# A fused two-block kernel on one core: large arrays at multiples of 2048 bytes, blocks of L stored block-wise and loaded by one transfer, every DMA issued by SyncE

## Chip, core and metric

The kernel runs on one core of a Trainium2 chip. The metric is the device time of one execution in microseconds; lower is better. Three runs of the kernel before the change are at hand, and one profiled execution, whose times count from the start of its span.

## What is computed

Two transformer blocks run one after the other on one sequence of 256 tokens with 2048 channels, all in float32. The first has chunked attention beside a multi-scale pool, and a gated feed-forward with a small convolution (`w_in`, `w_o`, `w_up`, `w_down`). The second has an RWKV-7 mixer and then a differential attention (`a_w_in`, `a_w_out`, `w_k_shared`, `w_v_shared`, `b_w_qg`, `b_w_out`). What matters here is the RWKV-7 part, whose recurrence over the tokens is

```
def step(S, inp):
    r_t, w_t, k_t, v_t, kk_t, a_t = inp
    sa = jnp.einsum('bhvk,bhk->bhv', S, kk_t)
    S = (S * w_t[:, :, None, :]
         - sa[..., None] * (kk_t * a_t)[:, :, None, :]
         + v_t[..., None] * k_t[:, :, None, :])
    y = jnp.einsum('bhvk,bhk->bhv', S, r_t)
    return S, y
```

for 32 heads of 64 channels. `a` is a sigmoid of a low-rank product (rank 96), the decay comes from a second one, and `kk` is `k` times a gain, normalized over each head by the root of its sum of squares.

## The kernel before

**Products.** Every large product is made from weights that are streamed from memory in units of 128 x 4 x 256 floats (512 KB; some of 384 KB). Each weight is split into two float32r parts: ScalarE copies `raw_w` into `w_hi` (L1046, in the woven stage L1336), VectorE writes `w_lo = raw_w - w_hi` (L1495, L1879) into the place of `raw_w`. The activations are split alike (`A..H`, `A..L`, side by side in one buffer). TensorE takes for each 128 x 128 block of a unit one matmul of `w_hi` on 512 columns (both parts, L636) and one of `w_lo` on 256 columns (the high part, L637): a unit is 8 such pairs. There are 8 places for raw units and 4 for `w_hi`. So SyncE may issue the weights of unit n when TensorE has finished unit n - 8, and ScalarE may split unit n when TensorE has finished unit n - 4. Each engine runs through its own program in order and waits at semaphores.

**The woven stage.** The products of the RWKV-7 mixer for `r`, `v` and `g` are 96 units (`NW`), written out unit by unit in one loop over n on each engine, and everything that the recurrence needs beforehand is put between the units at given n:
- The low-rank products: `lora_first` behind unit 7 of TensorE and `lora_second` (L794, matmuls L803) behind unit 15. The second makes 16 groups into three banks, and a bank comes free when ScalarE has taken the sigmoid of it (`sigmoids`, L1271, placed at n == 19, behind the square root of the norms). VectorE takes the reciprocal of the norms at n == 19 (`kk_rows`), and the result is wanted behind unit 20.
- For each of the 16 feature tiles f, with `prep_at(f) = 20 + 9f//4`, TensorE makes the triangular blocks of L for 8 (chunk, head) pairs (`lt_product`, L832, behind unit `prep+8`), ScalarE copies them to one of two small buffers (`lt_out`, L1302, at `prep+10`, which first waits until the store of tile f - 2 has landed), and SyncE stores them to `lt_dram` (`store_lt`, L475, at `prep+20`; two DMAs).
- L is then wanted with its 128 (tile, chunk, head) triples on the partitions. SyncE loads it with `load_lt` (L457), two DMAs of 8 partitions a tile: the first 15 tiles behind the weights of n = 73, the last one at n = 74.
- VectorE inverts the two 32 x 32 diagonal blocks of all 128 matrices at once in 31 steps of two operations each (`inverse_step`, L1861; the lines L1867 and L1870). The first step waits for all loads. The steps are spread over 21 units from n = 67:

```
        INVERSE_FROM = 67

        def inverse_steps(n):

            return range(max(0, n - INVERSE_FROM) * 31 // 21, min(max(0, n + 1 - INVERSE_FROM), 21) * 31 // 21)
```

Within its turn n VectorE first makes `w_lo` of the unit, then an evacuation (L1533, every fourth n), then the work of the tiles, then the steps of the inverse.
- Behind the weights of the last unit SyncE waits for the inverse, stores it (L520) and loads it block by block for the recurrence (`load_t`, L471), which follows the woven stage and uses small matmuls (L863).

**Queues.** SyncE issues the weights, the inputs, the scratch traffic and the output. GpSimd issues the constants at the start (L548, L549, L556), four side arrays of the attention (L565, behind the split of the first operand), the pool's weights (L568, behind the first product) and the distances and an expansion matrix (L613, L615).

**Memory.** The arrays are laid one behind another in each partition: the parameters (702 floats), the constants (896 floats), `w_lo`/`raw_w`, `w_hi`, two small arrays of 48 floats together, `x`, and so on.

## Time and profile before

| | |
|---|---|
| median of 3 runs | 2550.43 us (2547.89 to 2554.88) |
| profiled execution | 2553.74 us, of it span 2551.9 us |
| TensorE busy | 2353.8 us, 15826 matmuls |
| VectorE busy | 1490.3 us |
| ScalarE busy | 1093.7 us |
| GpSimd busy | 52.6 us |
| mean DMA traffic | 149 GB/s |

Busy time of TensorE is from the start of a matmul to its modelled end, and successive matmuls overlap, so a full TensorE is not one at its peak. "Granted clock" is the share of full clock that TensorE got: 1.00 is 2.4 GHz, and the lower level is 1.2 GHz. The chain that ended last goes back from the last instruction to what released it, or to the one before it on its engine. In the rows, PE is TensorE, DVE VectorE, ACT ScalarE, and SPq the queue of SyncE.

### The profile page before, as it was taken

The numbers are of one execution on the slowest core, as the hardware profiler recorded it, in microseconds if no ns is written. First come the engines' busy times: TensorE is split into PE (matmuls) and PEld (weight loads), VectorE is DVE, ScalarE is ACT, GpSimd is POOL, SyncE is SP. The second block draws the span as 40 slices with busy tenths as digits, with TensorE's granted clock in tenths as the row PEclk, the third lists the DMA queues.
The fourth block names the chain that finished last, engine by engine and source line by source line (L and its number), as shares of the span: only waits on it lengthen the run. The fifth ranks groups of instructions, "written<-read, shape, count | busy, mean of one in ns | idle before, by whom it ended". The sixth has DMA issues, their size and how long they took to land.

```text
span 2551.9 us, 41854 instructions
## 1 busy us (share of the span) xinstructions
PE 2353.8 (92%) x15826; PEld 1983.6 (78%) x15826; DVE 1490.3 (58%) x2024; ACT 1093.7 (43%) x1489; POOL 52.6 (2%) x61
## 2 busy tenths in 40 slices
PE   7997988999999999996999995999898899999797
PEld 6886777888888888885877775888477788887486
DVE  5555457775577657758735684722454544444754
ACT  4443435554444434442446452322333544444533
POOL 0003000000000000000000000000010000000100
PEclk9998999999999999997999997999889999999898
DMA  7662444565666656562644456400344455665052
GB/s 251 186 184 74 133 132 139 183 188 184 186 185 185 188 183 188 167 188 85 212 141 140 147 161 117 148 9 11 101 140 131 149 189 182 188 184 162 1 163 68
DMA packets 395775, 379.69 MB, mean 149 GB/s; under 512 B 41889, under 2 KB 394145, under 8 KB 394961
## 3 DMA queue, kind: packets, MB, share of 16 engines
q1 hardware_dynamic: 394690, 373.72, 47.9%
q0 software_dynamic: 976, 4.46, 0.5%
q8 instruction: 75, 1.23, 0.2%
q14 instruction: 34, 0.28, 0.0%
HBM read 370.79 MB, written 7.34 MB: 148 GB/s over the span
## 4 chain that ended last, share of the span: by engine, by line
PE 84%; DVE 9%; ACT 2%; issue 1%; DMA 1%; SPq 1%; POOL 0%; DVEq 0%; ACTq 0%; POOLq 0%
PE acc L636 48%; PE acc L637 24%; PE acc L863 3%; PE aux L863 2%; PE aux L676 1%; PE aux L686 1%; DVE w_lo L1879 1%; PE aux L809 1%; DVE w_lo L1495 1%; SPq L461 1%; DVE inverse L1870 1%; PE aux L803 1%; PE aux L786 1%; DVE outer L1867 1%; DVE y L1576 1%
## 5 line engine op out<-in xcount | busy, mean ns | idle before, releaser
L1495 DVE TENSOR_TENSOR w_lo<-raw_w,w_hi 128x1024 fp32r<-128x1024 f32 (+1 forms) x592 | 710.3, 1209 | 633.3 <-ACT w_hi L1046 631.5
L1046 ACT ACTIVATE w_hi<-raw_w 128x1024 fp32r<-128x1024 f32 (+1 forms) x592 | 618.4, 1049 | 852.6 <-PE acc L637 848.9
L636 PE MATMUL acc<-h,w_hi 128*128 128x512 f32 x1920 | 683.2, 399 | 23.7 <-DVE w_lo L1495 16.4
L637 PE MATMUL acc<-h,w_lo 128*128 128x256 f32 x1920 | 541.4, 282 | 0.0
L636 PEld LDWEIGHTS acc<-h,w_hi 128*128 128x128 f32 x1920 | 363.2, 189 | 113.8 <-issue 24.1
L636 PE MATMUL acc<-x_split,w_hi 128*128 128x512 f32 x1024 | 363.5, 399 | 8.7 <-DVE x_split L2004 8.7
L637 PEld LDWEIGHTS acc<-h,w_lo 128*128 128x128 f32 x1920 | 362.6, 189 | 0.0
L637 PE MATMUL acc<-x_split,w_lo 128*128 128x256 f32 x1024 | 288.4, 282 | 0.0
L636 PE MATMUL acc<-ff,w_hi 128*128 128x512 f32 x704 | 249.5, 398 | 1.0 <-DVE ff L1702 1.0
L636 PEld LDWEIGHTS acc<-x_split,w_hi 128*128 128x128 f32 x1024 | 193.3, 189 | 56.8 <-issue 9.0
L636 PE MATMUL acc<-xs_a,w_hi 128*128 128x512 f32 x512 | 190.6, 412 | 25.6 <-DVE xs_a L1753 21.3
L636 PE MATMUL acc<-xs_b,w_hi 128*128 128x512 f32 x512 | 186.9, 406 | 27.6 <-DVE w_lo L1879 26.9
L637 PE MATMUL acc<-ff,w_lo 128*128 128x256 f32 x704 | 197.8, 281 | 0.0
L637 PEld LDWEIGHTS acc<-x_split,w_lo 128*128 128x128 f32 x1024 | 193.1, 189 | 0.0
L636 PEld LDWEIGHTS acc<-ff,w_hi 128*128 128x128 f32 x704 | 132.4, 188 | 34.0 <-DVE ff L1702 1.3
L1879 DVE TENSOR_TENSOR w_lo<-raw_w,w_hi 128x1024 fp32r<-128x1024 f32 x96 | 116.5, 1222 | 70.9 <-ACT w_hi L1336 69.8
L637 PE MATMUL acc<-xs_a,w_lo 128*128 128x256 f32 x512 | 145.9, 285 | 0.0
L637 PE MATMUL acc<-xs_b,w_lo 128*128 128x256 f32 x512 | 145.0, 283 | 0.0
L636 PEld LDWEIGHTS acc<-xs_a,w_hi 128*128 128x128 f32 x512 | 98.4, 192 | 58.7 <-issue 31.1
L636 PEld LDWEIGHTS acc<-xs_b,w_hi 128*128 128x128 f32 x512 | 97.6, 191 | 57.9 <-DVE w_lo L1879 28.5
L1336 ACT ACTIVATE w_hi<-raw_w 128x1024 fp32r<-128x1024 f32 x96 | 100.2, 1053 | 85.0 <-PE acc L637 72.4
L637 PEld LDWEIGHTS acc<-ff,w_lo 128*128 128x128 f32 x704 | 132.2, 188 | 0.1
(304 smaller groups left out, 2942.2 us busy)
## 6 DMA issues: line engine op xcount, KB each, us to landing
raw_w<-in_w_up SPq DMA_DIRECT2D x176, 512.0 KB, 3.6
raw_w<-in_a_w_in SPq DMA_DIRECT2D x128, 512.0 KB, 3.6
raw_w<-in_w_in SPq DMA_DIRECT2D x64, 512.0 KB, 3.6
raw_w<-in_w_down SPq DMA_DIRECT2D x64, 512.0 KB, 3.5
raw_w<-in_b_w_qg SPq DMA_DIRECT2D x64, 512.0 KB, 3.6
raw_w<-in_w_o SPq DMA_DIRECT2D x32, 512.0 KB, 3.6
raw_w<-in_a_w_out SPq DMA_DIRECT2D x32, 512.0 KB, 4.3
raw_w<-in_w_k_shared SPq DMA_DIRECT2D x32, 512.0 KB, 3.6
```

The lines of the kernel that those rows point to most:

```text
L461: sp.dma_start(LT[8 * f:8 * f + 8, b, :, :], lt_dram[8 * f:8 * f + 8, b * H:(b + 1) * H, b * H:(b + 1) * H])\
L636: pe.matmul(out, wh, op[:, kt, :, :].rearrange("p h t -> p (h t)"), start=first, stop=False)
L637: mm = pe.matmul(out[:, 0:T], wl, op[:, kt, 0, :], start=False, stop=last)
L676: mm = pe.matmul(bank[:, 0:T], ONES, x[:, ds(4 * i + k, 1), :], start=(isinstance(i, int) and i == 0 and k == 0), stop=last)
L686: mm = pe.matmul(AUX[0][:, 0:T], ONES, SQB[0][:, j % 2, k, :], start=(j + k == 0), stop=(j + k == 6))
L786: mm = pe.matmul(AUX[w][0:LORA, 0:T], W1S[:, w, k, :], x[:, k, :], start=(k == 0), stop=(k == KD - 1))
L803: mm = pe.matmul(AUX[(0, 1, 3)[j % 3]][:, x * T:(x + 1) * T], W2S[:, w, f * P:(f + 1) * P], LOW[:, w, :], start=True, stop=True)
L863: mm = pe.matmul(bank[64 * h_:64 * h_ + 64, i * n:(i + 1) * n], lhs(h_, i), rhs(h_, i), start=(start and i == 0), stop=(stop and i == 3))
L1046: act.activation(WHI[:, q, 0:ku, :], RAWW[:, u, 0:ku, :], ACT.Copy).then_inc(hi_made, 1)
L1336: act.activation(WHI[:, n % 4, :, :], RAWW[:, slot, :, :], ACT.Copy).then_inc(hi_made, 1)
L1495: dve.tensor_tensor(WLO[:, u, 0:ku, :], RAWW[:, u, 0:ku, :], WHI[:, q, 0:ku, :].bitcast(F32), ALU.subtract)\
L1879: dve.tensor_tensor(WLO[:, slot_of(n), :, :], RAWW[:, slot_of(n), :, :], WHI[:, n % 4, :, :].bitcast(F32), ALU.subtract)\
```

## The change

The change has six parts. (1) The two small arrays go ahead of the weights, with a filler of 368 floats, and the reserve for DMAs that software describes shrinks from 8192 to 2048 bytes; the large arrays then start at multiples of 2048 bytes. (2) `lt_dram` has the shape of `LT`, (128, 2, 32, 32). A tile is stored with four DMAs, one for each head and diagonal block, three units earlier; all of `LT` is loaded with one DMA behind the weights of n = 71, once all stores have landed. (3) The inverse starts at n = 69 and its 31 steps are spread over 20 units. (4) The DMAs of GpSimd are issued by SyncE: the constants ahead of the first weights, `scan` and the side arrays behind the weights of `w_in`, the pool's weights behind the first 8 units of `w_o`, the last two behind the weights of `a_w_out`. (5) ScalarE takes the sigmoids at n == 18 and the square root after them. (6) The waits are adapted.

```
@@ -170,11 +170,12 @@
         HEADSEL = CF[:, CCOL["headsel"]:CCOL["headsel"] + CHUNK]
         PAIRSEL = CF[:, CCOL["pairsel"]:CCOL["pairsel"] + CHUNK]
         STACK = CF[:, CCOL["stack"]:CCOL["stack"] + CHUNK]
+        OMU, OKA = sb(root, "one_minus_mu", [P, 2 * KD]), sb(root, "one_minus_k_a", [P, KD])
+        sb(root, "pad_to_10k", [P, 368])
         with ExitStack() as same_place:
             WLO = sb(same_place, "w_lo", [P, RAW, KU, UNIT_COLS], F32R)
         RAWW = sb(root, "raw_w", [P, RAW, KU, UNIT_COLS])
         WHI = sb(root, "w_hi", [P, SPL, KU, UNIT_COLS], F32R)
-        OMU, OKA = sb(root, "one_minus_mu", [P, 2 * KD]), sb(root, "one_minus_k_a", [P, KD])
         X = sb(root, "x", [P, KD, T])
         FOLD = sb(root, "fold", [P, 4, T])
 
@@ -402,15 +403,16 @@
 
         PREP = {prep_at(f): f for f in range(KD)}
         PAIRS = {pair_at(s_, p): (s_, p) for s_ in (1, 2) for p in range(8)}
-        INVERSE_FROM = 67
+        INVERSE_FROM, INVERSE_OVER = 69, 20
 
         def inverse_steps(n):
 
-            return range(max(0, n - INVERSE_FROM) * 31 // 21, min(max(0, n + 1 - INVERSE_FROM), 21) * 31 // 21)
+            done = [min(max(0, x - INVERSE_FROM), INVERSE_OVER) * (H - 1) // INVERSE_OVER for x in (n, n + 1)]
+            return range(*done)
 
         def by_chunk(x):
             return x.rearrange("p (c t) -> p c t", c=NCH)
-        lt_dram, t_dram, x_dram = dram("lt_scratch", (P, CHUNK, CHUNK)), dram("t_scratch", (P, 2, H, H)), dram("x_scratch", (P, KD, T))
+        lt_dram, t_dram, x_dram = dram("lt_scratch", (P, 2, H, H)), dram("t_scratch", (P, 2, H, H)), dram("x_scratch", (P, KD, T))
 
         def small(m, n):
 
@@ -445,8 +447,22 @@
             for q in range(4):
                 sp.dma_start(X[:, 4 * q:4 * q + 4, :], h["x_t"][4 * q * P:4 * (q + 1) * P].rearrange("(k p) t -> p k t", p=P))\
                   .then_inc(x_in[q], 16)
+            sp.dma_start(CF[:, 0:NFIX], h["consts"][:, 0:NFIX]).then_inc(const_in, 16)
+            sp.dma_start(CF[:, NFIX:], h["consts"][:, CCOL["tri"]:CCOL["expand"]]).then_inc(const_in, 16)
             weights(8, lambda i, b: (w_in, i * 512 + b * 256))
-            weights(4, lambda i, b: (h["w_o"][0], i * 512 + b * 256))
+
+            sp.dma_start(SCAN[:, :], h["consts"][:, CCOL["scan"]:CCOL["scan"] + T]).then_inc(scan_in, 16)
+            sp.wait_ge(operand, 4)
+            band0 = CCOL["band"]
+            for dst, src in ((HANK[:, :, :], h["bias_rows"]),
+                             (FLIP[:, :], h["consts"][:, CCOL["flip"]:CCOL["flip"] + P]),
+                             (BAND[:, :, :], h["consts"][:, band0:band0 + 2 * T].rearrange("p (q t) -> p q t", q=2)),
+                             (INVC[:, :, :], h["consts"][:, CCOL["invcount"]:CCOL["invcount"] + 4 * T].rearrange("p (g t) -> p g t", g=4))):
+                sp.dma_start(dst, src).then_inc(side, 16)
+            weights(1, lambda i, b: (h["w_o"][0], i * 512 + b * 256))
+            sp.wait_ge(acc_free, 4 + 32)
+            sp.dma_start(POOLW[:, :, :, :], h["pool_w"][0].rearrange("g (c p) d -> p g c d", p=P)).then_inc(pool_w_in, 16)
+            weights(3, lambda i, b: (h["w_o"][0], i * 512 + (512 + b * 256)))
             for t0, tiles in GROUPS:
                 weights(tiles // 2, lambda i, b: (w_up, i * 256 + (t0 * P + b * FF)))
                 weights(4, lambda i, b: (w_down, i * 512 + b * 256), ku=tiles // 4, kt0=t0)
@@ -454,13 +470,6 @@
 
             sp.wait_ge(x_ready, 8)
             sp.dma_start(x_dram, X[:, :, :]).then_inc(x_spilled, 16)
-            def load_lt(f):
-
-                sp.wait_ge(lt_stored[f % 2], 32 * (f // 2 + 1))
-                for b in range(2):
-                    sp.dma_start(LT[8 * f:8 * f + 8, b, :, :], lt_dram[8 * f:8 * f + 8, b * H:(b + 1) * H, b * H:(b + 1) * H])\
-                      .then_inc(inv_in, 16)
-
             def load_t(n):
                 g, c = STEPS[n]
                 m = n % 2
@@ -474,9 +483,11 @@
 
             def store_lt(f):
                 sp.wait_ge(lt_ready, f + 1)
+                dst = lt_dram[8 * f:8 * f + 8].rearrange("(c h) b s t -> h b s c t", h=2)
                 for hh in range(2):
-                    dst = lt_dram[8 * f:8 * f + 8].rearrange("(c h) s t -> h s c t", h=2)[hh]
-                    sp.dma_start(dst, (XS, US)[f % 2][64 * hh:64 * hh + 64, :, :]).then_inc(lt_stored[f % 2], 16)
+                    for b in range(2):
+                        at = 64 * hh + H * b
+                        sp.dma_start(dst[hh, b], (XS, US)[f % 2][at:at + H, :, H * b:H * b + H]).then_inc(lt_stored[f % 2], 16)
 
             def woven_weights(n):
 
@@ -508,13 +519,12 @@
                 if n == 16:
                     lora_weights_2()
                 woven_weights(n)
-                if n - 20 in PREP:
-                    store_lt(PREP[n - 20])
-                if n - 21 in PREP and n - 21 > 51:
-                    load_lt(PREP[n - 21])
-                if n == 73:
-                    for f in range(15):
-                        load_lt(f)
+                if n - 17 in PREP:
+                    store_lt(PREP[n - 17])
+                if n == 71:
+                    for even_odd in lt_stored:
+                        sp.wait_ge(even_odd, 64 * KD // 2)
+                    sp.dma_start(LT[:, :, :, :], lt_dram).then_inc(inv_in, 16)
             seen(unit_done, NW)
             sp.wait_ge(inverted, 1)
             sp.dma_start(t_dram, TT[:, :, :, :]).then_inc(t_stored, 16)
@@ -531,6 +541,11 @@
             sp.wait_ge(bon_done, KD)
             sp.dma_start(X[:, :, :], x_dram).then_inc(x_back, 16)
             weights(4, lambda i, b: (h["a_w_out_2"][0], i * 512 + b * 256))
+
+            sp.wait_ge(gn_ready, KD)
+            sp.dma_start(DIST[:, :, :], h["consts"][:, CCOL["dist"]:CCOL["dist"] + 2 * T].rearrange("p (q t) -> p q t", q=2))\
+                .then_inc(dist_in, 16)
+            sp.dma_start(EXP5[:, :], h["consts"][0:32, CCOL["expand"]:CCOL["expand"] + D // 2]).then_inc(dist_in, 16)
             for w in (h["w_k_shared_2"], h["w_v_shared_2"]):
                 weights(4, lambda i, b: (w, i * 512 + b * 256))
             weights(8, lambda i, b: (h["b_w_qg_2"][0], i * 512 + b * 256))
@@ -545,28 +560,14 @@
         @block.gpsimd
         def _(pool):
             seen = Counts(pool)
-            pool.dma_start(CF[:, 0:NFIX], h["consts"][:, 0:NFIX]).then_inc(const_in, 16)
-            pool.dma_start(CF[:, NFIX:], h["consts"][:, CCOL["tri"]:CCOL["expand"]]).then_inc(const_in, 16)
             pool.sem_inc(unit_done, RAW)
             pool.sem_inc(acc_free, 4)
             pool.sem_inc(sq_free, 2)
             pool.sem_inc(sc_free, 2)
 
 
-            pool.dma_start(SCAN[:, :], h["consts"][:, CCOL["scan"]:CCOL["scan"] + T]).then_inc(scan_in, 16)
             pool.memset(LOW[LORA:LORA + 1, :, :], 1.0).then_inc(low_one, 1)
             pool.wait_ge(low_one, 1)
-            pool.wait_ge(operand, 4)
-            band0 = CCOL["band"]
-            for dst, src in ((HANK[:, :, :], h["bias_rows"]),
-                             (FLIP[:, :], h["consts"][:, CCOL["flip"]:CCOL["flip"] + P]),
-                             (BAND[:, :, :], h["consts"][:, band0:band0 + 2 * T].rearrange("p (q t) -> p q t", q=2)),
-                             (INVC[:, :, :], h["consts"][:, CCOL["invcount"]:CCOL["invcount"] + 4 * T].rearrange("p (g t) -> p g t", g=4))):
-                pool.dma_start(dst, src).then_inc(side, 16)
-
-            pool.wait_ge(acc_free, 4 + 32)
-            pool.dma_start(POOLW[:, :, :, :], h["pool_w"][0].rearrange("g (c p) d -> p g c d", p=P)).then_inc(pool_w_in, 16)
-
             def link(ins):
                 ins.then_inc(gstep, 1)
                 pool.wait_ge(gstep, seen(gstep))
@@ -609,10 +610,6 @@
                 pool.tensor_tensor(gnt(1, f), gnt(1, f), G4[:, f, :], ALU.mult).then_inc(gn_gated, 1)
 
 
-            pool.wait_ge(gn_ready, KD)
-            pool.dma_start(DIST[:, :, :], h["consts"][:, CCOL["dist"]:CCOL["dist"] + 2 * T].rearrange("p (q t) -> p q t", q=2))\
-                .then_inc(dist_in, 16)
-            pool.dma_start(EXP5[:, :], h["consts"][0:32, CCOL["expand"]:CCOL["expand"] + D // 2]).then_inc(dist_in, 16)
             for n in range(8):
                 pool.wait_ge(o_out, n + 1)
                 pool.tensor_tensor(Q5[:, 2 * n:2 * n + 2, :], Q5[:, 2 * n:2 * n + 2, :], G5[:, 2 * n:2 * n + 2, :], ALU.mult).then_inc(o_gated, 1)
@@ -1269,12 +1266,12 @@
                 act.activation(KFR[:, f % 3, :], K[:, f, :], ACT.Square, scale=PV[:, c:c + 1]).then_inc(kk_sq, 1)
 
             def sigmoids():
-                act.wait_ge(kk_summed, KD)
-                act.activation(INVR[:, :], AUX[2][0:32, 0:T], ACT.Sqrt).then_inc(kk_norm, 1)
                 for j in range(KD):
                     act.wait_ge(lora_done, j + 1)
                     act.activation((KAP, BET)[j % 2][:, j // 2 * 2:j // 2 * 2 + 2, :],
                                    AUX[(0, 1, 3)[j % 3]][:, :].rearrange("p (x t) -> p x t", x=2), ACT.Sigmoid).then_inc(sig_ready, 1)
+                act.wait_ge(kk_summed, KD)
+                act.activation(INVR[:, :], AUX[2][0:32, 0:T], ACT.Sqrt).then_inc(kk_norm, 1)
 
             def k_factor(f):
                 c = COL["a_k_a_2"] + f
@@ -1303,7 +1300,7 @@
                 p = f % 2
                 act.wait_ge(lt_done, f + 1)
                 if f >= 2:
-                    act.wait_ge(lt_stored[p], 32 * (f // 2))
+                    act.wait_ge(lt_stored[p], 64 * (f // 2))
                 act.activation((XS, US)[p][:, :, :], by_chunk(AUX[1][:, 0:T]), ACT.Copy)\
                    .then_inc(lt_ready, 1)
 
@@ -1345,7 +1342,7 @@
                 if 8 <= n < 16:
                     kk_square(2 * (n - 8))
                     kk_square(2 * (n - 8) + 1)
-                if n == 19:
+                if n == 18:
                     sigmoids()
                 if n - 10 in PREP:
                     lt_out(PREP[n - 10])
@@ -1861,7 +1858,7 @@
             def inverse_step(s_):
                 n, r = s_ + 1, H - 1 - s_
                 if s_ == 0:
-                    dve.wait_ge(inv_in, 32 * KD)
+                    dve.wait_ge(inv_in, 16)
                     dve.wait_ge(inv_init, 1)
                 o = OUTER[:, 0:2 * n * r].rearrange("p (b j t) -> p b j t", b=2, j=n)
                 link(dve.tensor_tensor(o, LT[:, :, s_:s_ + 1, s_ + 1:].broadcast_to([P, 2, n, r]),
@@ -2098,7 +2095,7 @@
     rows = x["rel_bias"][0][:, np.clip(distance, -P, P) + P]
     arrays["bias_rows"] = np.ascontiguousarray(rows.transpose(1, 0, 2))
 
-    nc = _bacc.Bacc("TRN2", target_bir_lowering=False, num_devices=1, dynamic_dma_scratch_size=8192)
+    nc = _bacc.Bacc("TRN2", target_bir_lowering=False, num_devices=1, dynamic_dma_scratch_size=2048)
     h = {n: nc.dram_tensor("in_" + n, a.shape, F32, kind="ExternalInput").ap() for n, a in arrays.items()}
     h["out"] = nc.dram_tensor("out_t", (D, T), F32, kind="ExternalOutput").ap()
     program(nc, h)
```

## Rows read from the trace of the kernel before

**Rows 1.** The profile's page: the chain that ended last, by engine.

```profile
PE 84%; DVE 9%; ACT 2%; issue 1%; DMA 1%; SPq 1%; POOL 0%; DVEq 0%; ACTq 0%; POOLq 0%
```

**Rows 2.** Waits of the whole span: total us, times, longest us.

```profile
DVE outer L1867 <- DMA lt_blocks<-lt_scratch: 31.3, 1, 31.3
PE acc L636 <- DVE w_lo L1879: 29.0, 6, 25.5
```

**Rows 3.** Timeline of SyncE's queue, 1538 to 1585 us: start, length, what.

```profile
1539.17 1.26 SPq L479 DMA_DIRECT2D lt_scratch<-wkv_x  x2
...
1547.12 18.56 SPq L461 DMA_DIRECT2D lt_blocks<-lt_scratch  x30
```

**Rows 4.** Timeline of VectorE, 1573 to 1578 us; in brackets the idle before.

```profile
1574.19 0.23 DVE L1867 TENSOR_TENSOR outer<-lt_blocks,inverse 128x62 f32<-128x62 f32 x1 [31.31 <-DMA lt_blocks<-lt_scratch]
```

**Rows 5.** Timeline of TensorE, 1549 to 1586 us.

```profile
1575.99 0.79 PE L636 MATMUL acc<-xs_b,w_hi 128*128 128x512 f32 x1 [25.55 <-DVE w_lo L1879]
...
1576.79 0.63 PE L636 MATMUL acc<-xs_b,w_hi 128*128 128x512 f32 x1
...
1577.43 0.63 PE L636 MATMUL acc<-xs_b,w_hi 128*128 128x512 f32 x1
...
1582.33 0.40 PE L636 MATMUL acc<-xs_b,w_hi 128*128 128x512 f32 x1
1582.57 0.28 PE L637 MATMUL acc<-xs_b,w_lo 128*128 128x256 f32 x1
1582.69 0.39 PE L636 MATMUL acc<-xs_b,w_hi 128*128 128x512 f32 x1
```

**Rows 6.** Timeline of TensorE, 1340 to 1368 us: the second low-rank product.

```profile
1343.42 2.86 PE L803 MATMUL aux<-lora_low,raw_w 97*128 97x256 f32 x12
1351.18 14.24 PE L803 MATMUL aux<-lora_low,raw_w 97*128 97x256 f32 x52 [4.90 <-ACT r_kappa L1276]
```

**Rows 7.** Timelines of ScalarE and TensorE, 1430 to 1440 us.

```profile
1435.05 0.39 ACT L1307 ACTIVATE wkv_u<-aux 128x256 f32<-128x256 f32 x1 [5.25 <-DMA lt_scratch<-wkv_u]
...
1438.79 0.51 PE L636 MATMUL acc<-xs_a,w_hi 128*128 128x512 f32 x1 [1.74 <-DVE w_lo L1879]
```

**Rows 8.** DMA issues: count, KB each, median us from issue to landing.

```profile
lt_scratch<-wkv_x SPq DMA_DIRECT2D x16, 64.0 KB, 3.3
...
t_scratch<-inverse SPq DMA_DIRECT2D x1, 1024.0 KB, 6.5
inverse_blocks<-t_scratch SPq DMA_DIRECT2D x64, 16.0 KB, 1.8
```

**Rows 9.** VectorE's groups, 1574 to 1636 us: count | busy us, mean ns.

```profile
L1879 DVE TENSOR_TENSOR w_lo<-raw_w,w_hi 128x1024 fp32r<-128x1024 f32 x22 | 26.9, 1224 | 0.7
L1870 DVE TENSOR_TENSOR inverse<-inverse,outer 128x62 f32<-128x62 f32 (+15 forms) x31 | 16.4, 528 | 1.1
L1867 DVE TENSOR_TENSOR outer<-lt_blocks,inverse 128x62 f32<-128x62 f32 (+15 forms) x31 | 16.2, 522 | 31.7 <-DMA lt_blocks<-lt_scratch 31.3
L1533 DVE SCALAR_TENSOR_TENSOR silu_g<-acc,fold 128x512 f32<-128x512 f32 x5 | 3.4, 684 | 0.0
```

**Rows 10.** Waits of SyncE's queue from 1370 to 1550 us.

```profile
SPq L491 <- PE acc L637: 135.3, 49, 3.7
```

**Rows 11.** Timeline of ScalarE, 1341 to 1366 us: a split, table load, sigmoid.

```profile
1342.20 1.06 ACT L1336 ACTIVATE w_hi<-raw_w 128x1024 fp32r<-128x1024 f32 x1 [0.18 <-DMA raw_w<-in_a_w_in]
...
1349.23 1.28 ACT L1276 ACT_TABLE_LOAD   x1
...
1363.72 0.60 ACT L1276 ACTIVATE beta<-aux 128x512 f32<-128x512 f32 x1 [0.27 <-PE aux L803]
```

**Rows 12.** Timeline of ScalarE, 13 to 16 us: the first weights.

```profile
13.94 1.06 ACT L1046 ACTIVATE w_hi<-raw_w 128x1024 fp32r<-128x1024 f32 x1 [2.31 <-DMA raw_w<-in_w_in]
15.43 1.06 ACT L1046 ACTIVATE w_hi<-raw_w 128x1024 fp32r<-128x1024 f32 x1 [0.44 <-DMA raw_w<-in_w_in]
```

**Rows 13.** The page's costliest groups: matmuls on the first operand.

```profile
L636 PE MATMUL acc<-h,w_hi 128*128 128x512 f32 x1920 | 683.2, 399 | 23.7 <-DVE w_lo L1495 16.4
```

81 lines of the change are left out of this document (40 added, 41 removed).

## The prediction, made before the changed kernel was run

> **What bounds the kernel now.** I read the page's first and fourth parts, the table of waits, and then, in the stretch that the waits pointed at, the timelines of TensorE, VectorE, ScalarE and of the queue on SyncE. The page says that TensorE is busy for nine tenths of a span of 2551.9 us and carries 84% of the chain that ended last [rows 1]. So an edit pays only where TensorE stands still, or where it makes TensorE itself faster. The waits show one such place above all: 31.3 us in which VectorE waits for the load of `lt_blocks`, and in its wake 29.0 us, all its times together, in which TensorE waits for `w_lo` [rows 2].
>
> The queue shows why. Behind unit 73 it issues 30 of the 32 loads of `lt_blocks` in 18.56 us [rows 3]; weights and the last two loads come after them. VectorE wants these blocks in its turn for unit 67, for the first of 31 elimination steps, and in its program order the `w_lo` of unit 68 stands behind them. It gets them at 1574.19 [rows 4]. TensorE stands still for 25.55 us and starts again at 1575.99 [rows 5]. It comes back at the lower of its two levels, 1.2 GHz: one pair of matmuls (a 128x512 on `w_hi`, a 128x256 on `w_lo`) takes 0.64 us from start to start; some 6 us later, at 2.4 GHz, it is 0.35 us [rows 5] (2.82 us for the 8 pairs of a unit, so 0.353 more exactly).
>
> The second place is the second low-rank product, L803: 12 matmuls in 2.86 us, a gap of 4.90 us until the first sigmoid, then 52 in 14.24 us [rows 6]. A third is small: one store of `lt_scratch` landed late, ScalarE waited 5.25 us for it, and TensorE lost 1.74 us [rows 7].
>
> **The change, part by part.**
>
> *Blocks loaded by one transfer.* 32 loads go, one of 1 MB comes. The scratch array now has the shape of `LT`, so it is one contiguous row for each of 128 partitions. The nearest row is the 1 MB store of the inverse, 6.5 us to landing [rows 8]. Count from the end of TensorE's unit 62. SyncE then issues unit 70 and the last four stores; two of today's, of 256 pieces each, take 1.26 us to issue [rows 3], so four with half the pieces some 2 us. They land 3.3 us behind issue [rows 8], so all is stored about 5.5 us after unit 62. The load then lands 6.5 us later, at 12 us. VectorE asks for it behind `w_lo` of unit 69, which cannot be made before unit 65 is done (3 x 2.82 = 8.5 us) plus 1.05 us for `w_hi` and 1.2 us for `w_lo`: 10.7 us. It waits 1 to 2 us, while TensorE has units 66 to 69 ready, some 6 us of cover beyond that. No stall is left. This takes out 25.55 us. It also takes out the slow restart: from 1575.99 to 1582.33 only 10 pairs ran, in 6.34 us instead of 3.53 us: 2.8 us.
>
> *31 steps over 20 units from 69, instead of 21 from 67.* In the stretch of the steps VectorE has 16.4 + 16.2 us of steps, 22 subtractions of 1.224 us and 3.4 us of joins [rows 9], with hardly a gap: it is full. For 21 units it needs 16.4 + 16.2 + 25.7 + 3.4 = 61.7 us (less small overlaps) where TensorE needs 59.3; for 20 units 60.5 against 56.5. The 4 us that it falls behind are under the lead that it starts with, which the stalled kernel did not have. Before, TensorE had three gaps of some 0.4 us here; I take 0.7 us afterwards in place of 1.3. Bounds: a gain of 1.3, a loss of 3. The inverse ends one unit, 2.8 us, later. Its store (6.5 us) and the first loads (1.8 us) [rows 8] still end before TensorE's last unit, because SyncE issues that store only behind the weights of unit 95, that is, when unit 87 is done, with 8 units left.
>
> Stall, restart and steps: 25.55 + 2.8 + 0.6 = 29.0 us.
>
> *Stores by blocks, earlier.* Two stores of 256-byte pieces become four of 128-byte pieces (64 issues for 32); the number of pieces is the same. SyncE issues them three units earlier (17 instead of 20 behind the tile's first). By then ScalarE's copy is done, since it follows the product behind unit `prep+8` and SyncE's place is the end of unit `prep+9`: nothing new blocks weights behind it. The issues add 16 x 0.7 = 11 us to a queue that waits 135.3 us for TensorE between 1370 and 1550 [rows 10]. That is the cover. The nearest row for such pieces is `inverse_blocks`: 128-byte pieces, 16 KB, 1.8 us [rows 8]. The buffer is wanted again two tiles on, 3.5 units or more behind the issue, over 12 us. So the 1.74 us go. The Trainium skill, "DMA: Bandwidth & Descriptors", Specifications, speaks against the smaller pieces: below 512 bytes a DMA does not run at line rate. By that rule a store would land no sooner though it carries half the bytes; at the old 3.3 us the sum stays as it is.
>
> *Sigmoids at n = 18, the square root behind them.* Before, ScalarE waits for the weights of unit 19, splits them, evacuates, loads a table, takes the root and loads a second table from 1349.23 on [rows 11]; the first sigmoid follows at 1350.5, 7 us behind the first product. Now the sigmoids follow the split of unit 18 (1342.20 + 1.06) and one table load of 1.28 us [rows 11]: first one at 1344.6, done at 1345.1, before TensorE's fourth group (three banks are free at the start). After that ScalarE keeps a pace of 0.865 us (0.60 and 0.27 us idle) [rows 11], so TensorE sets it: 16 x 0.865 = 13.9 us. Before it was 22.0 us from 1343.42 to 1365.4. Gain 7.7 us (4.9 of gap, the rest is the low level after it). What is late next: the root, then the reciprocal on VectorE, both wanted behind unit 20; they are ready near 1365, unit 20 ends near 1371. The split of unit 19 comes out near 1362.5 with its unit due at 1365.5. Bounds: 4.9 to 8 us.
>
> *DMAs from GpSimd to SyncE.* At the start SyncE issues the two constant loads between x and the weights: two issues of 0.55 us, a gap-free queue behind 2 MB of x. TensorE starts when the first weights, landed at 13.94 [rows 12], are split. The same bytes stand ahead of them, but for the 128 KB of `scan`, which now come later, worth 0.4 us at the 0.5 MB in 1.5 us of the weights' landings [rows 12]. I take -0.4 us, bounds -1.5 to +1.5. The other loads follow the last `w_in` weights (25 us before the attention wants them), the pool's waits for the same evacuation as before, and the last two are wanted 450 us later: nothing.
>
> *Arrays at multiples of 2048 bytes.* No row of this trace sets two start addresses against each other. What the trace shows is that a matmul on `w_hi` takes 399 ns on the mean over the 1920 of `h` [rows 13], as it does in the woven stage at the upper level [rows 5], though what VectorE, ScalarE and the DMAs do beside it differs. I take 0. The bounds are wide and are the rivals C and D. The Trainium skill, "DMA: Bandwidth & Descriptors", How a descriptor splits into AXI transactions, would favour it: pieces off a 256-byte boundary cost extra beats, an estimated 36 for 32 on a 1 KB row. By that the weights at the start would land 1.3 us sooner; elsewhere DMA is hidden.
>
> **Sum:** 29.0 + 1.7 + 7.7 + 0.4 = 38.8 us. The profiled execution took 2553.74 us for a span of 2551.9; it would take 2514.9. The median of the runs is 3.3 us lower, 2550.43, so the forecast is 2511.6 us.
>
> **Rivals.**
> A. *The blocks still come late.* The load hangs on all 64 stores, the last of them issued behind unit 70. If store and load together take 22 us, not 12, VectorE drains its cover and TensorE stops again for 4.5 us and then runs behind a full VectorE: 12 us of the 29.0 are lost, 2524. For it: VectorE is full; against it: the two landings measured [rows 8]. 8%.
> B. *The sigmoids give nothing*, because the root that now comes last is waited for, or ScalarE's late split of unit 19 is: 2519. Two to four us of slack speak against it. 6%.
> C. *The matmuls get faster by alignment.* At 2.4 GHz 768 columns take 320 ns, the pair takes 353 [rows 5]. If all of that went, the 5440 pairs of the large products would give 180 us: 2332. Against it: the excess grows with the columns (0.24 and 0.12 us for 512 and 256) [rows 5], as a rate does and a bad start address doesn't. 6%.
> D. *Slower: with all large arrays at the same place modulo 2048, TensorE's reads of operand and weights, or those of other engines, collide.* Place: every pair. It decides from 38.8 us / 5440 = 7 ns a pair, 2% of 353. For a price, the only row with slower pairs is the low level; a twentieth of the way from 353 to 640 is 14 ns, 76 us in all less the gains: 2588. Against it: today's constant rate beside changing company. 5%.
> E. *The wait stays*: another semaphore, for instance that of the stores, holds VectorE or SyncE as long as before; only the sigmoids and the small stall are gained: 2541. 3%.
>
> **Numbers.** The forecast case has 72%, its own range is 2505 to 2519. With A and B the range is 2500 to 2526, which leaves out C, D and E. A measurement of this kernel tells 0.3% (7.7 us) from nothing: faster 0.93, same 0.03, slower 0.04.
>
> **What would show it.** In the profile afterwards: no wait of VectorE for `lt_blocks` over 3 us; no gap of TensorE over 2 us between unit 16 and unit 95 of the woven stage; one load of `lt_blocks` of 1 MB; L803's 64 matmuls in about 14 us at one clock; no wait of ScalarE for `lt_scratch`; the first `w_hi` near 13.5 us. A pair that is not 353 ns makes the prediction wrong in one way, a full VectorE with gaps in TensorE near units 78 to 88 in the other.

## The result, and the profile after

The changed kernel takes 2484.9 us (median of 4 runs, 2476.6 to 2492.0) against 2549.9 us before on the same chip (4 runs, 2547.9 to 2554.9): a ratio of 0.974, 95% interval 0.970 to 0.978. The forecast was 2511.6 us with a range from 2500, so the kernel is faster by 27 us more than I said and lies 15 us below my range. The profiled execution took 2489.8 us for a span of 2487.7. Two things are to be read: the steps that I had costed came out nearly as costed in their sum (40.3 us against 38.8, in the run with the old layout below), and the step that I had costed at nothing is worth 22 us or somewhat more.

First the steps that were costed. The page's chain by engine, against [rows 1]:

```profile
PE 87%; DVE 9%; ACT 2%; issue 1%; DMA 0%; POOL 0%; SPq 0%; DVEq 0%; ACTq 0%; POOLq 0%
```

The waits of the whole span (total, times, longest), against [rows 2]:

```profile
PE acc L633 <- DVE w_lo L1876: 0.8, 1, 0.8
...
DVE outer L1864 <- DMA lt_blocks<-lt_scratch: 0.2, 1, 0.2
```

31.3 us of waiting for `lt_blocks` have become 0.2 us, and in their wake TensorE's 29.0 us of waiting for `w_lo` have become 0.8. The queue on SyncE and VectorE after it (timelines of 1495 to 1520 us; [rows 3, 4] before):

```profile
1505.51 1.94 SPq L490 DMA_DIRECT2D lt_scratch<-wkv_u  x4
1507.91 0.39 SPq L502 DMA_DIRECT2D raw_w<-in_a_w_in  x1
1509.55 0.34 SPq L527 DMA_DIRECT2D lt_blocks<-lt_scratch  x1
...
1516.15 0.23 DVE L1864 TENSOR_TENSOR outer<-lt_blocks,inverse 128x62 f32<-128x62 f32 x1 [0.21 <-DMA lt_blocks<-lt_scratch]
```

From the issue of the last four stores to VectorE's first step are 10.6 us; I had worked out 12 us from unit 62 on. The page's DMA issues give the landings, against [rows 8]:

```profile
lt_blocks<-lt_scratch SPq DMA_DIRECT2D x1, 1024.0 KB, 6.6
t_scratch<-inverse SPq DMA_DIRECT2D x1, 1024.0 KB, 6.3
inverse_blocks<-t_scratch SPq DMA_DIRECT2D x64, 16.0 KB, 1.8
lt_scratch<-wkv_x SPq DMA_DIRECT2D x32, 16.0 KB, 2.6
```

The second low-rank product (timelines of TensorE, then of ScalarE, 1320 to 1340 us; [rows 6, 11] before) has its 64 matmuls in one piece. The first sigmoid comes 1.16 us behind the first of them, and the root is last:

```profile
1322.91 14.08 PE L800 MATMUL aux<-lora_low,raw_w 97*128 97x256 f32 x64
...
1322.74 1.28 ACT L1271 ACT_TABLE_LOAD   x1
1324.07 0.60 ACT L1271 ACTIVATE r_kappa<-aux 128x512 f32<-128x512 f32 x1
1324.94 0.60 ACT L1271 ACTIVATE beta<-aux 128x512 f32<-128x512 f32 x1 [0.27 <-PE aux L800]
...
1337.64 1.28 ACT L1274 ACT_TABLE_LOAD   x1
1338.93 0.38 ACT L1274 ACTIVATE kk_inverse_rows<-aux 32x256 f32<-32x256 f32 x1
```

Now the place where the rest of the gain is. The page's groups for the matmuls of `w_hi`, for the first operand [rows 13 before] and the last large one:

```profile
L633 PE MATMUL acc<-h,w_hi 128*128 128x512 f32 x1920 | 669.8, 393 | 23.0 <-DVE w_lo L1492 15.7
...
L633 PE MATMUL acc<-x_split,w_hi 128*128 128x512 f32 x1024 | 363.2, 400 | 8.6 <-DVE x_split L2001 8.6
```

On `h` a matmul has gone from 399 to 393 ns; on `x_split` it has not (400). The view by windows counts matmuls, and that is the sharper reading: it gives busy time (and count) of the line's matmuls and of its weight loads, the granted clock, the DMA share and GB/s. Line L636 before:

```profile
450.00:1050.00 600.00, 600.00 (x1699) 319.22 (x1698) 1.00 0.60 185
1990.00:2260.00 270.00, 270.00 (x765) 143.63 (x764) 1.00 0.60 185
```

Line L633 after:

```profile
450.00:1050.00 600.00, 600.00 (x1731) 323.62 (x1732) 1.00 0.61 188
1990.00:2260.00 270.00, 270.00 (x765) 143.62 (x765) 1.00 0.61 186
```

In the same 600 us TensorE takes 32 more pairs, at the same granted clock of 1.00 (2.4 GHz) and with nearly the same DMA share (0.61 against 0.60); in the other stretch it takes as many as before. From the start times: before, a pair is 353.3 ns from start to start, everywhere. After, it is either 346.7 ns (three pairs in 1040 ns) or 353.3 ns (three in 1060 ns), and the level holds without an exception through each stretch of 60 pairs or more in which TensorE isn't interrupted. The level can change between stretches without any fall of the clock: stretches of 63 pairs that start at 1185, 1209 and 1232 us run at 346.7, 353.4 and 346.7 ns, and the granted clock is 1.00 from 1170 to 1735 us. The mean over all pairs goes from 353.3 to 349.3 ns; times 5440 pairs that is 22 us.

### The profile page after: what moved, and what is told of

Same layout as the page of the kernel before. It is cut to its first block, busy times and chain, and to the rows that moved or that the text cites. A ratio compares the mean times of both kernels' runs of the same rounds, so it can differ in the third digit from the quotient of the medians.

```text
span 2487.7 us, 41832 instructions
## 1 busy us (share of the span) xinstructions
PE 2324.1 (93%) x15826; PEld 1970.7 (79%) x15826; DVE 1489.4 (60%) x2024; ACT 1092.7 (44%) x1489; POOL 46.7 (2%) x51
## 4 chain that ended last, share of the span: by engine, by line
PE 87%; DVE 9%; ACT 2%; issue 1%; DMA 0%; POOL 0%; SPq 0%; DVEq 0%; ACTq 0%; POOLq 0%
PE acc L633 49%; PE acc L634 25%; PE acc L860 3%; PE aux L860 3%; PE aux L673 1%; PE aux L806 1%; PE aux L683 1%; DVE w_lo L1492 1%; PE aux L800 1%; PE aux L783 1%; DVE y L1573 1%; PE aux L946 0%; DVE inverse L1867 0%; DVE diff_scores L2043 0%; DVE w_lo L1876 0%
## 5 line engine op out<-in xcount | busy, mean ns | idle before, releaser
L633 PE MATMUL acc<-h,w_hi 128*128 128x512 f32 x1920 | 669.8, 393 | 23.0 <-DVE w_lo L1492 15.7
L634 PE MATMUL acc<-h,w_lo 128*128 128x256 f32 x1920 | 537.7, 280 | 0.0
L633 PEld LDWEIGHTS acc<-h,w_hi 128*128 128x128 f32 x1920 | 361.1, 188 | 103.9 <-issue 23.4
L633 PE MATMUL acc<-x_split,w_hi 128*128 128x512 f32 x1024 | 363.2, 400 | 8.6 <-DVE x_split L2001 8.6
L634 PEld LDWEIGHTS acc<-h,w_lo 128*128 128x128 f32 x1920 | 364.1, 190 | 0.0
L634 PE MATMUL acc<-x_split,w_lo 128*128 128x256 f32 x1024 | 288.1, 281 | 0.0
L633 PE MATMUL acc<-ff,w_hi 128*128 128x512 f32 x704 | 245.3, 393 | 1.1 <-DVE ff L1699 1.1
L633 PEld LDWEIGHTS acc<-x_split,w_hi 128*128 128x128 f32 x1024 | 193.1, 189 | 57.3 <-issue 9.0
L633 PE MATMUL acc<-xs_a,w_hi 128*128 128x512 f32 x512 | 189.7, 412 | 23.6 <-DVE xs_a L1750 21.4
L634 PE MATMUL acc<-ff,w_lo 128*128 128x256 f32 x704 | 196.9, 280 | 0.0
L634 PEld LDWEIGHTS acc<-x_split,w_lo 128*128 128x128 f32 x1024 | 194.1, 190 | 0.0
L633 PE MATMUL acc<-xs_b,w_hi 128*128 128x512 f32 x512 | 183.4, 402 | 1.5 <-DVE w_lo L1876 0.8
L633 PEld LDWEIGHTS acc<-ff,w_hi 128*128 128x128 f32 x704 | 131.8, 187 | 30.9 <-DVE ff L1699 1.5
L1876 DVE TENSOR_TENSOR w_lo<-raw_w,w_hi 128x1024 fp32r<-128x1024 f32 x96 | 116.5, 1221 | 62.5 <-ACT w_hi L1333 61.1
L634 PE MATMUL acc<-xs_a,w_lo 128*128 128x256 f32 x512 | 145.2, 284 | 0.0
L634 PE MATMUL acc<-xs_b,w_lo 128*128 128x256 f32 x512 | 143.5, 280 | 0.0
L633 PEld LDWEIGHTS acc<-xs_a,w_hi 128*128 128x128 f32 x512 | 98.3, 192 | 56.4 <-issue 30.9
L634 PEld LDWEIGHTS acc<-ff,w_lo 128*128 128x128 f32 x704 | 132.9, 189 | 0.1
L633 PEld LDWEIGHTS acc<-xs_b,w_hi 128*128 128x128 f32 x512 | 96.2, 188 | 30.4 <-issue 5.5
```

The lines of the kernel that those rows point to most:

```text
L633: pe.matmul(out, wh, op[:, kt, :, :].rearrange("p h t -> p (h t)"), start=first, stop=False)
L634: mm = pe.matmul(out[:, 0:T], wl, op[:, kt, 0, :], start=False, stop=last)
L1876: dve.tensor_tensor(WLO[:, slot_of(n), :, :], RAWW[:, slot_of(n), :, :], WHI[:, n % 4, :, :].bitcast(F32), ALU.subtract)\
```

## The experiments

Levels below are of the pair, start to start. "Distance" is where the operands of the large products start minus where the weights start, in bytes modulo 256. The kernel before has the weights at 384 and the operands at 576 modulo 2048 (distance 192); the changed one has both at 0.

**The parts one by one.** First the layout alone, on the kernel before:

```
+        OMU, OKA = sb(root, "one_minus_mu", [P, 2 * KD]), sb(root, "one_minus_k_a", [P, KD])
+        sb(root, "pad_to_10k", [P, 368])
         with ExitStack() as same_place:
             WLO = sb(same_place, "w_lo", [P, RAW, KU, UNIT_COLS], F32R)
...
         WHI = sb(root, "w_hi", [P, SPL, KU, UNIT_COLS], F32R)
-        OMU, OKA = sb(root, "one_minus_mu", [P, 2 * KD]), sb(root, "one_minus_k_a", [P, KD])
...
-    nc = _bacc.Bacc("TRN2", ..., dynamic_dma_scratch_size=8192)
+    nc = _bacc.Bacc("TRN2", ..., dynamic_dma_scratch_size=4096)
```

> The kernel before with the large arrays at multiples of 2048 bytes and nothing else (reserve 4096 instead of 8192 bytes, so that the filler fits; weights start at 12,288). Theory (the start addresses set the rate of the matmul pairs): stretches with 346.7 ns a pair appear, the time falls by 15 to 30 us against before, ratio about 0.990 to 0.994. Rival (the pair rate comes from the other edits, the moved DMAs for instance): every pair stays at 353 ns and the time is that of before within 0.3%.

Measured: 2519.7 us (2512.6 to 2529.9) beside 2547.7 of before, ratio 0.988 (0.986 to 0.990). The mean pair is 349.2 ns. 28 us come from the layout alone: the fall is inside the 15 to 30 us that I expected, the ratio just under the 0.990 to 0.994 that I had written beside it. (This edit also halves the reserve; further down only pads move, and the levels move with them.) (The profiled execution, 2529.9 us, was the slowest of the four; its 4.1 ns a pair are 22 us.)

The reverse, the changed kernel with the arrays put back (no pad, the two small arrays behind `w_hi`, a DMA scratch of 8192):

> The changed kernel with the old layout (weights at 14,720, operands 576 bytes past a multiple of 2048). Theory: all pairs at 353 ns, time near the blind forecast, 2508 to 2516 us, ratio 0.984 to 0.987. Rival: pairs at 347 ns remain and the time stays near 2485 us.

Measured: 2507.3 us (2505.3 to 2509.1), ratio 0.984 (0.982 to 0.985), 353.3 ns in every stretch. This is the kernel that my sum described; it said 2511.6. Against the 2547.7 us of before beside it, 40.3 us are gained where the sum had 38.8. The first starts of some products say where the gain lies:

| first start, us | before | blocks alone | sigmoids alone | changed, old layout |
|---|---|---|---|---|
| L803's product | 1343.4 | 1340.3 | 1342.7 | 1340.8 |
| first blocks of L | 1405.9 | 1403.1 | 1397.3 | 1395.3 |
| scan, first product | 1661.7 | 1626.4 | 1653.6 | 1618.7 |
| end | 2551.9 | 2514.1 | 2543.8 | 2506.9 |

The stage of the sigmoids is 8.0 us shorter (62.5 to 54.5), the woven stage 32.4 us (255.8 to 223.4), what stands behind it 2.0 us, what stands ahead 2.6 us. Ahead of L803 the blocks alone, which change nothing there, came 3.1 us earlier too: these last two are the scatter of one execution.

Blocks alone (the one-transfer load, the stores by blocks, 20 units from 69, on the kernel before):

> The kernel before with the block-wise stores, the one load and the steps over 20 units from 69 alone. My sum gives 29.0 + 1.7 us: 2519 us, ratio 0.988, no gap of TensorE over 1 us in units 60 to 95. Rival (the wait for the blocks stays in another form): 2540 us or more.

Measured: 2517.2 us (2515.9 to 2518.4), ratio 0.988 (0.986 to 0.990), 30.4 us less than 2547.7.

Sigmoids alone (called at `n == 18`, the root behind them):

> The kernel before with the sigmoids at n == 18 and the root behind them alone. My sum gives 7.7 us: 2542 us, ratio 0.997, the 64 matmuls of the second low-rank product in 14 us without a gap. Rival (the stall at unit 67 swallows the gain, or the root is waited for): 2550 us.

Measured: 2543.2 us, 10 runs, ratio 0.998 (0.997 to 0.999). The stall of the blocks is all there, in TensorE's timeline:

```profile
1567.94 0.79 PE L636 MATMUL acc<-xs_b,w_hi 128*128 128x512 f32 x1 [25.75 <-DVE w_lo L1879]
```

Its profile shows 7.9 us gained in the stage itself, the medians 4.5 us (the interval allows 1.8 to 6.9, so 7.7 is outside). Where the difference goes I did not find; the moved DMAs have no run of their own. Both together are bounded: 2517.2 - 2507.3 = 9.9 us.

**Which address?** In each of the next runs only pads differ from the changed kernel. The first two move one side. The operands 576 bytes on:

```
         WHI = sb(root, "w_hi", [P, SPL, KU, UNIT_COLS], F32R)
+        sb(root, "pad_operands", [P, 144])
```

> The changed kernel with only the operands of the large products (x_split, mix, ff, wkv_out, h, xs_a, xs_b) moved by 576 bytes, back to their old place modulo 2048; w_hi and w_lo stay at multiples of 2048. Theory M (what counts is where the moving operand starts, since its 256 columns are the rows that TensorE streams... the operand is the stationary side or the moving side of every matmul alike): pairs of 353.3 ns throughout and some 2507 us, as with the old layout. Theory W (what counts is where the weights start): the fast stretches of 346.7 ns stay, the mean pair is near 349.3 ns and the time between 2476 and 2492 us. If each side gives a part: a mean pair between 349.3 and 353.3, some 2496 us.

The weights 384 bytes on, the operands at a multiple of 2048 as they were:

```
-        sb(root, "pad_to_10k", [P, 368])
+        sb(root, "pad_to_10k", [P, 368 + 96])
...
+        sb(root, "pad_operands", [P, 512 - 96])
```

> The mirror image: w_lo and w_hi start at 384 modulo 2048, their old place, and the operands stay at multiples of 2048. Theory W (the weights' start counts): pairs of 353.3 ns throughout, some 2507 us. Theory M (the operands' start counts): fast stretches of 346.7 ns stay, 2476 to 2492 us. A third reading, that both sides have to be aligned at once, gives 2507 us here and in the run with the operands moved.

Measured: 2508.0 us (2494.8 to 2513.6) and 2497.3 us (2494.2 to 2498.8). Neither theory holds. With the operands moved the levels are 348.9 and 353.3 ns; with the weights moved there is one level, 351.1 ns, in all stretches. It matters where both sides stand, taken together. The window view for the second, line L634:

```profile
450.00:1050.00 600.00, 600.00 (x1710) 320.88 (x1710) 1.00 0.61 187
1990.00:2260.00 270.00, 270.00 (x770) 144.43 (x769) 1.00 0.61 187
```

Then both sides moved together, by 1024, by 128 (`+ 32`), and by 576 bytes (`+ 144`):

```
-        sb(root, "pad_to_10k", [P, 368])
+        sb(root, "pad_to_10k", [P, 368 + 256])
```

> The changed kernel with its pad longer by 1024 bytes, so that all large arrays start at 1024 modulo 2048. If the multiple of 2048 itself matters: pairs of 353.3 ns, some 2507 us. If a smaller multiple (256, 512, 1024) is enough: nothing changes, mean pair near 349.3 ns and 2476 to 2492 us. I think the second likelier, 3 to 1.

> The changed kernel with its pad longer by 128 bytes: all large arrays start at 128 modulo 2048, which is where the old layout's weights stood modulo 256. If a multiple of 256 bytes or more is what counts: pairs of 353.3 ns throughout, some 2507 us. If a multiple of 128 or 64 is enough and it was the order of the arrays that mattered: near 349.3 ns, 2476 to 2492 us.

> The changed kernel with its pad longer by 576 bytes: weights and operands all start at 576 modulo 2048, the place of the operands in the old layout. If only the distance between weights and operands modulo 2048 counts: levels 346.7 and 353.3 ns as at 0, 128 and 1024, between 2476 and 2509 us. If the start address itself counts down to 64 bytes: another level, and with 353.3 throughout some 2507 us.

Measured: 2486.2 us (2482.1 to 2491.2), 2504.3 us (2493.4 to 2508.9) and 2495.7 us (2493.8 to 2500.5). All three have the two levels of the changed kernel, 346.7 and 353.3 ns, and differ in which stretches have which. So no multiple of 2048, 1024 or 256 is needed for the fast level to appear. But the times are not alike: 2482.1 to 2491.2 us with both at 1024, 2493.4 to 2508.9 with both at 128, run beside each other. In the profiles, the two longest stretches are both slow with both sides at 128 and at 576, while one of the two is fast at 1024. More on this under what stays open.

**Is the level fixed or drawn?** The changed kernel, the same program once more (no edit):

> The changed kernel once more, nothing in the program changed. Theory R (the level of the pair, 346.7 or 353.3 ns, is a state of a kernel with weights and operands at the same place modulo 2048 that is drawn anew at disturbances): the same two levels, but in other stretches than in the first profile; x_split, all slow there, may be fast here; any time between 2476 and 2492 us. Rival (the level is fixed by the addresses of each stage): the same stretches at the same levels, x_split at 353.3 and h at 346.7 ns, 2485 to 2492 us.

Measured: 2492.5 us. Line L633:

```profile
450.00:1050.00 600.00, 600.00 (x1699) 319.06 (x1698) 1.00 0.60 186
1990.00:2260.00 270.00, 270.00 (x780) 145.67 (x779) 1.00 0.62 190
```

The two stretches have changed places: 1699 where the first profile had 1731, and 780 where it had 765. The same program has the levels in other places, so they are not fixed by the addresses of a stage: the level is drawn when TensorE starts again and is then kept. The interruption can be very short: with the operands at 576, one pair that took 367 ns in place of some 349, at 1577.5 us, was enough to change 348.9 into 353.3 ns. Two stretches matter most, because nothing interrupts them: 1931 pairs from 392 us (12.9 us between the levels) and 1018 pairs from 1924 us (6.8 us). Draws of this size can make most of the scatter of the changed kernel, 2476.6 to 2492.5 us, but not all of it: from 349.2 to 350.5 ns, the mean pairs of the two profiled executions, are 7 us over 5440 pairs, and the executions are 2.7 us apart. The levels of the executions without a profile are not known.

**The distance.** Four more with only the operands moved, `pad_operands` being `[P, 64]`, `[P, 32]`, `[P, 48]` and `[P, 56]`:

> The changed kernel with only the operands moved by 256 bytes against the weights. If what counts is the distance of operands and weights modulo 256: as the changed kernel, levels 346.7 and 353.3 ns, 2476 to 2509 us. If it is the distance modulo 512 or more: a level in between (349 to 351 ns in some stretch, as at 384 and 576), 2494 to 2508 us.

> The changed kernel with only the operands moved by 128 bytes against the weights. If the distance modulo 128 or less counts: levels 346.7 and 353.3 ns, 2476 to 2509 us. If the distance modulo 256 or more counts: a level in between, 2494 to 2508 us.

> The changed kernel with only the operands moved by 192 bytes against the weights, the distance that the old layout has modulo 256. Theory D: 353.3 ns in every long run of pairs and 2505 to 2509 us, though weights and operands both stand at multiples of 64 and the weights at a multiple of 2048. Rival (aligned weights give part of the gain in themselves): a level under 353, 2490 to 2500 us.

> The changed kernel with only the operands moved by 224 bytes against the weights, 32 bytes short of the same place modulo 256. On a straight line from 346.7 ns at 0 by 2.22 ns for 64 bytes it would be 354.4 ns, some 2512 us; if the levels stop at 353.3 ns: some 2507 us; if it goes by nearness to 256: 347.8 ns and 2480 to 2508 us.

Measured: 2483.4 us (2479.4 to 2487.7), 2496.2 us (2493.8 to 2497.4), 2510.5 us (2504.3 to 2511.0) and 2501.7 us (2499.5 to 2506.1). At 256 the kernel behaves as at 0, and in the layouts below too the level goes by the distance modulo 256. At 192, the old distance, it is at 353.3 ns although the weights stand at a multiple of 2048 (the time is 1.5 us over the 2505 to 2509 that I expected): aligned weights alone give nothing. 128 is 351.1 ns again, as with the weights at 384 and the operands at 0, which is 128 modulo 256 too. And at 32 bytes (`[P, 8]`):

> The changed kernel with only the operands moved by 32 bytes against the weights. The lower level so far is 346.7 ns at distance 0, 348.9 at 64, 351.1 at 128 and 353.3 at 192, 2.22 ns for 64 bytes. If it goes in a straight line: 347.8 ns where the run is fast. If it goes in steps of 64 bytes: 346.7 or 348.9. Open is whether the upper level of 353.3 is drawn as well: with it 2480 to 2508 us, without it 2478 to 2484 us.

Measured: 2476.4 us (2474.1 to 2478.8), ratio 0.971 (0.969 to 0.973), and 346.7 ns in every long stretch. The slow level was not drawn once, and there is no 347.8 ns: the straight line of my expectation is refuted, and the time lies 1.6 us under the 2478 to 2484 that went with the single level. Was that luck? The same edit, once more:

> The changed kernel with the operands moved by 32 bytes, once more and with more runs. If the single fast level is a property of this distance: 346.7 ns in every long run again, and times within 5 us of each other, 2474 to 2479 us. If the first profile was a lucky draw: stretches of 353.3 ns, and a scatter up to 2492 us as in the changed kernel.

Measured: 2475.1 us (5 runs, 2472.9 to 2476.0), ratio 0.9704 (0.969 to 0.972). Line L634, both stretches fast, as in the first run at 32:

```profile
450.00:1050.00 600.00, 600.00 (x1732) 324.92 (x1732) 1.00 0.60 188
1990.00:2260.00 270.00, 270.00 (x780) 146.20 (x780) 1.00 0.61 189
```

**Without any aligned array.** The kernel before, with one small array between weights and operands, of 64 bytes, then of 96 (`[P, 24]`):

```
         OMU, OKA = sb(root, "one_minus_mu", [P, 2 * KD]), sb(root, "one_minus_k_a", [P, KD])
+        sb(root, "pad_operands", [P, 16])
```

> The kernel before with one array of 64 bytes put behind one_minus_k_a, so that the operands move from 576 to 640 modulo 2048, and the weights stay at 384: no large array is at a multiple of 2048, 1024, 512 or 256, but operands and weights are now at the same place modulo 256. Theory D (only the distance of operand and weights modulo 256 sets the levels of the pair): levels of 346.7 and 353.3 ns, each kept through a run of pairs without a break, and 2512 to 2540 us, as with the new layout alone. Rival (alignment itself): 353.3 ns throughout, 2548 to 2552 us.

> The kernel before with one array of 96 bytes behind one_minus_k_a: operands 32 bytes past the weights' place modulo 256, no large array at a multiple of 256. Theory D (only the distance modulo 256 counts): 346.7 ns in every long run of pairs, as in the changed kernel with the operands at 32; 5440 pairs by 6.6 ns are 35.9 us, so 2514 us, with little scatter. Rival (the single fast level at 32 needs aligned weights): both levels, or another, 2520 to 2550 us.

Measured: 2531.8 us (2521.9 to 2542.6), both levels; and 2521.5 us (2515.2 to 2528.7), 346.7 ns (some stretches 346.9) in every long one, though no array is at a multiple of 256. The levels go by the distance in both layouts. The time is 7.5 us over my 2514: the old stall is longer in this kernel, in TensorE's timeline.

```profile
1554.55 0.80 PE L637 MATMUL acc<-xs_b,w_hi 128*128 128x512 f32 x1 [28.60 <-DVE w_lo L1880]
```

That is 3.05 us more than the 25.55 us before [rows 5]: a TensorE that is faster only waits longer for the blocks. It does not explain all of the 7.5 us.

All runs by distance; a level is the mean of a long stretch (60 pairs or more):

| distance | levels seen, ns | kernels: median us |
|---|---|---|
| 0 | 346.7 and 353.3 | changed 2484.9; again 2492.5; all at 1024: 2486.2; all at 128: 2504.3; all at 576: 2495.7; operands at 256: 2483.4; layout alone 2519.7; old layout and 64 bytes 2531.8 |
| 32 | 346.7 only | operands at 32: 2476.4, 2475.1; old layout and 96 bytes 2521.5 |
| 64 | 348.9 and 353.3 | operands at 576: 2508.0 |
| 128 | 351.1 only | operands at 128: 2496.2; weights at 384: 2497.3 |
| 192 | 353.3 only | changed, old layout 2507.3; operands at 192: 2510.5; before 2549.9; blocks alone 2517.2; sigmoids alone 2543.2 |
| 224 | 346.7 and 353.3 | operands at 224: 2501.7 |

The levels give the times. From 353.3 to 351.1 ns is 12 us over 5440 pairs: 2507.3 - 12 = 2495 (2496.2 and 2497.3 measured). From 353.3 to 346.7 is 36 us: 2471 (2475.1 and 2476.4 measured).

## Why the prediction was wrong

**What failed.** "Arrays at multiples of 2048 bytes. ... I take 0." By the medians the term is 2507.3 - 2484.9 = 22.4 us; by the ratios to the kernel before, each measured beside it (0.9837 and 0.9741), it is some 24.5 us; the layout alone gave 28 us. At the pair that is 353.3 - 349.3 = 4.0 ns on the mean of 5440, at an unchanged clock. I had seen that no row set two start addresses against each other, and took the steadiness of 353 ns under changing company as a reason for nothing. It was no reason: a constant distance gives a constant rate, and nothing in the trace of before varied it. I had this mechanism as rival C, and priced it as all or nothing, 180 us or 0. The argument against it was that the excess over 320 ns "grows with the columns, as a rate does and a bad start address doesn't". The second part is wrong: a fifth of the excess over 320 ns, 6.6 of 33.3 ns, does go by addresses. And the first part held only at the old distance. From start to start the two matmuls of a pair take 235.0 and 118.3 ns there, 230.0 and 116.7 at the fast level of distance 0, and 228.3 and 118.3 at distance 32: over the 213.3 and 106.7 ns of 512 and 256 columns at 2.4 GHz that is 21.7 and 11.7 ns, 16.7 and 10.0, 15.0 and 11.7. At distance 32 the whole gain is in the matmul of 512 columns. A bound from both sides would have put some of that between 2332 and 2511.6; with a range cut off at 2500 it had no room. My list of signs had named a pair that is not 353 ns as one way to be wrong, and that is the way it went. Multiples of 2048 are not the cause either: the fast level comes because operands and weights no longer stand 192 bytes apart modulo 256.

**What held**, by the changed kernel with the old layout:

- *Stall, restart, steps, small store stall:* 29.0 + 1.7 = 30.7 us forecast; 32.4 us in the stage's own times, 30.4 us for the blocks alone. Waiting for `w_lo` between the units of the woven stage one gap of 0.77 us is left where I said 0.7. Full VectorE, 31 steps over 20 units: no trouble, as said.
- *Stores:* four issues take 1.94 us (2 forecast), and they land in 2.6 us, not 3.3. I had the Trainium skill, "DMA: Bandwidth & Descriptors", Specifications, against the smaller pieces. No run here has the same bytes in larger pieces; what the trace shows is that quartered transfers in pieces half as long landed 0.7 us sooner, and it was hidden.
- *Sigmoids:* 7.7 us forecast (the terms of that sum, 22.0 - 13.9, make 8.1); 8.0 us of stage in the profile. L803's 64 matmuls take 14.08 us (14 forecast), the first sigmoid 1.16 us behind the first product (1.2). The root ends at 1339.3, nobody waits. Alone, the medians give 4.5 us, under my lower bound of 4.9, and where the rest goes stays open. That my sum comes within 1.5 us of the 40.3 measured is in part that: the sigmoids with the moved DMAs are worth 9.9 us behind the blocks, 8.1 forecast.
- *DMAs by SyncE:* 0.4 us forecast; no run has them alone, so the term itself is not shown. ScalarE's first split (two rows of its timeline in the changed kernel, against [rows 12]):

```profile
13.25 1.06 ACT L1043 ACTIVATE w_hi<-raw_w 128x1024 fp32r<-128x1024 f32 x1 [3.08 <-DMA raw_w<-in_w_in]
14.60 1.06 ACT L1043 ACTIVATE w_hi<-raw_w 128x1024 fp32r<-128x1024 f32 x1 [0.29 <-DMA raw_w<-in_w_in]
```

It starts 0.7 us earlier than before, with the old layout at 13.38 (0.56 us earlier); the kernel before with only the blocks changed started at 13.57, so most of this is scatter. The distance to the second split is 1.35 us; before and with the old layout it is 1.50. The Trainium skill, "DMA: Bandwidth & Descriptors", How a descriptor splits into AXI transactions, would have 36 beats for 32 on rows that start 128 bytes past a multiple of 256, an estimated 12%; the trace agrees, with 11% (the page speaks of reads, and here the shifted side is the one that is written). It does not agree elsewhere: with both sides at 576, which is 64 modulo 256, the page's count would be 34 beats, an estimated 6%, and the first splits are 1.51 us apart all the same. Only this stage at the start is paced by landings, so the 0.15 us bought little: the first split came 0.1 us earlier than with the old layout, which is within what the first split scatters between runs of one layout (12.97 and 13.25 us for the changed kernel).

**The rivals.** A (blocks late), B (sigmoids nothing) and E (the wait stays) are refuted by the rows above. D (slower by collisions) is refuted for this layout. That the levels go by a distance would fit reads that get in each other's way, but no run shows such a mechanism.

**What stays open.** Why 256; why the lower level rises by 2.2 ns for each 64 bytes of distance up to 192 and is back at 346.7 at 224, why 32 knows no slow level, and what decides the draw at 0: no run changed anything but addresses. Every pad also moved all arrays behind `w_hi`, so that the two addresses are those of TensorE's own two reads is the nearest reading, not an isolated one. One regularity is only noted: the stretch of 479 pairs at 36 us was fast in seven of the eight profiles at distance 0 and slow in the old layout with 64 bytes.

A second one says that the distance is not everything. At distance 0 the draw came out better where both sides also stood at multiples of 256. The thirteen executions of the changed kernel with both sides so placed (0, 256, 1024) take 2476.6 to 2492.5 us; the eight with both at 128 or at 576 take 2493.4 to 2508.9, and those with both at 128 ran beside those at 1024, those with both at 576 beside those at 256. In the profiles, at least one of the two longest stretches was fast in each of the five kernels at multiples of 256 (0 twice, 256, 1024, the layout alone), and neither in any of the three others (128, 576, the old layout with 64 bytes), with mean pairs of 347.8 to 350.5 against 351.7 to 351.9 ns. So absolute places seem to set the odds of the draw, and the distance the levels that can be drawn; eight profiles are too few to call it shown.

Not tried: other distances under 32, another distance between `w_lo` and `w_hi`, and a distance in the matmuls of the scan.

## What to carry to other kernels

In a kernel bound by TensorE with streamed weights, measure the start-to-start time of its main pair, and move the operand against the weights in steps of 32 or 64 bytes: one line of padding was worth 36 us by pair rate (34 us by the medians, 2510.5 at distance 192 to 2476.4 at 32, run beside each other), and the best distance here (32 bytes modulo 256) also took most of the scatter with it. The relation of the two addresses sets the levels; weights at a multiple of 2048 gave nothing at distance 192, and multiples of 256 for both seem to matter only for the odds at distance 0. And where the trace of before can't show an effect because nothing in it varies the cause, a steady number is no evidence for zero: keep part of the range for it.

A version that beats both kernels is the changed one with `pad_operands` of 32 bytes behind `w_hi`: 2475.1 us in the run with five, where 13 executions of the changed kernel and its two like-behaved shifts (all at 1024, operands at 256) lie between 2476.6 and 2492.5 us. Against the kernel before, measured beside each, the ratio is 0.9704 (0.969 to 0.972) for it and 0.974 (0.970 to 0.978) for the changed one.
